# Swapping 32-row halves of a rotary embedding with transfers instead of a matrix product, in an attention layer whose TensorE never rests

## The reference

```python
proj = h @ attn_w_in                       # 2048 -> queries, keys, values, gates
q = rmsnorm(q, q_gain); k = rmsnorm(k, k_gain)          # per head, over 128 features
# of each head: features 0-63 by the token's row, 64-127 by its column;
# in each 64: a = first 32, b = second 32
q = [a * cos - b * sin, b * cos + a * sin]              # the same for k
p = softmax(q @ k.T * scale)                            # then values, a gate, an output product
```

## Time and profile before

| | |
|---|---|
| median of 3 runs | 2449.05 us (2448.95 to 2449.17) |
| profiled execution, first to last instruction | 2448.6 us |
| what lies around the span, against the median | 0.45 us |
| PE busy | 2375.3 us, 97% |
| DVE busy | 1410.8 us, 58% |
| ACT busy | 1171.6 us, 48% |
| POOL busy | 246.5 us, 10% |
| DMA | 402.37 MB, 164 GB/s |

### The profile page before, as it was taken

One profiled execution on the slowest core, in us unless ns is written; L12 is line 12 of the kernel. 1 busy time (PEld: TensorE's weight loads), 2 busy tenths in 40 slices (PEclk: granted clock), 3 DMA queues, 4 the chain that ended last, 5 costly groups with the idle time before them and its releaser, 6 DMA issues.

```text
span 2448.6 us, 43575 instructions
## 1 busy us (share of the span) xinstructions
PE 2375.3 (97%) x17033; PEld 2200.1 (90%) x17033; DVE 1410.8 (58%) x1814; ACT 1171.6 (48%) x1739; POOL 246.5 (10%) x202
## 2 busy tenths in 40 slices
PE   8999999999989999999999989999999989999998
PEld 7897899998879999999988869998889989998876
DVE  5555644458566666666644457885554463555544
ACT  5444544445454444454444444444454453664443
POOL 0000000015001221221200001220002000010210
PEclk9999999999999999999999999999999999999999
DMA  8544466646646556556655545444335555553343
GB/s 288 154 138 134 133 190 186 181 153 199 203 132 195 183 176 193 188 175 192 202 187 188 189 146 159 149 153 121 96 103 173 171 179 164 150 155 104 104 146 138
DMA packets 254407, 402.37 MB, mean 164 GB/s; under 512 B 15136, under 2 KB 111389, under 8 KB 253245
## 3 DMA queue, kind: packets, MB, share of 16 engines
q1 hardware_dynamic: 252452, 393.53, 51.2%
q10 hardware_dynamic: 1832, 7.13, 0.8%
HBM read 396.38 MB, written 4.22 MB: 164 GB/s over the span
## 4 chain that ended last, share of the span: by engine, by line
PE 92%; DVE 4%; ACT 3%; issue 1%; DMA 0%; POOL 0%; ACTq 0%; DVEq 0%; SPq 0%; POOLq 0%
PE bank L1755 63%; PE bank L1852 13%; PE bank L2278 4%; PE bank L1770 2%; DVE wlo L1130 1%; PE bank L2244 1%; PE bank L2069 1%; ACT whi L569 1%; PE bank L2038 1%; PE bank L1795 1%; PE bank L2205 1%; PE bank L2013 0%; PE bank L2007 0%; PE bank L1917 0%; DVE mixtmp L1418 0%
## 5 line engine op out<-in xcount | busy, mean ns | idle before, releaser
L1130 DVE TENSOR_TENSOR wlo<-raw,whi 128x1024 fp32r<-128x1024 f32 x749 | 953.6, 1282 | 832.3 <-ACT whi L569 829.8
L1755 PE MATMUL bank<-ahi,whi 128*128 128x256 f32 (+1 forms) x4224 | 1215.7, 288 | 2.8 <-ACT gg L891 0.9
L1755 PE MATMUL bank<-ahi,wlo 128*128 128x256 f32 (+1 forms) x4224 | 1199.9, 284 | 0.0
L1755 PE MATMUL bank<-alo,whi 128*128 128x256 f32 (+1 forms) x4224 | 1197.4, 283 | 0.0
L569 ACT ACTIVATE whi<-raw 128x1024 fp32r<-128x1024 f32 x749 | 787.8, 1057 | 799.6 <-PE bank L1755 560.4
L1755 PEld LDWEIGHTS bank<-ahi,whi 128*128 128x128 f32 x4224 | 799.5, 189 | 20.0 <-issue 17.1
L1755 PEld LDWEIGHTS bank<-ahi,wlo 128*128 128x128 f32 x4224 | 798.5, 189 | 0.0
L1755 PEld LDWEIGHTS bank<-alo,whi 128*128 128x128 f32 x4224 | 796.2, 188 | 1.4 <-issue 0.2
L1852 PE MATMUL bank<-whi,ghi 128*128 128x512 f32 x352 | 139.0, 395 | 0.0
L1852 PE MATMUL bank<-whi,glo 128*128 128x512 f32 x352 | 139.0, 395 | 0.0
L1852 PE MATMUL bank<-wlo,ghi 128*128 128x512 f32 x352 | 139.0, 395 | 0.0
(11 more groups left out here) (305 smaller groups left out, 2303.8 us busy)
## 6 DMA issues: line engine op xcount, KB each, us to landing
raw<-in_w_up SPq DMA_DIRECT2D x176, 512.0 KB, 4.6
raw<-in_w_in SPq DMA_DIRECT2D x156, 512.0 KB, 3.6
raw<-in_attn_w_in SPq DMA_DIRECT2D x96, 512.0 KB, 3.9
raw<-in_gla_w_in SPq DMA_DIRECT2D x96, 512.0 KB, 3.7
raw<-in_w_down SPq DMA_DIRECT2D x80, 512.0 KB, 4.2
raw<-in_w_out SPq DMA_DIRECT2D x32, 512.0 KB, 4.2
raw<-in_attn_w_out SPq DMA_DIRECT2D x32, 512.0 KB, 3.6
raw<-in_gla_w_out SPq DMA_DIRECT2D x32, 512.0 KB, 3.5
```

The source lines that it names most:

```text
L1130: dve.tensor_tensor(wlo[:, u % RING, :], raw[:, u % RAW, :], whi[:, u % RING, :].bitcast(F32), ALU.subtract).then_inc(wlo_ready, 1)
L1755: mm = pe.matmul(bank[:, base + t, 0:T], w[wp][:, k, col:col + P], rhs(ap, k0 + k), start=begins and k == 0 and (wp, ap) == (0, 0), stop=e ...
```

## The change

The product with `turn` goes. In its place SyncE issues for every head four SBUF-to-SBUF transfers of 32 rows of 272 `fp32` elements (1088 bytes a row, 136 KB in all) from `n2` to a new tile `turned2`, each from the rows that lie 32 away. The signs of the matrix go into the `sin` table. `qk_rotate(p - 1)` moves on VectorE from the even step, ahead of the reciprocal, to the odd step behind it, and reads `turned2` instead of PSUM. The exchanges stand in SyncE's queue behind certain loads (those of odd units, eight units ahead of what VectorE splits), and SyncE waits there for `qk_normed` and `qk_sin`. The loops over trips of `aqk` and `ag` in SyncE's program are unrolled. The wait for the tables goes from TensorE to VectorE. Some semaphores of the start are merged into others without a change of order.

```diff
-    turn = np.zeros((P, P), f32)
...
+    sign = np.where(np.arange(P) % 64 < 32, f32(-1.0), f32(1.0))[:, None]
...
-        "c_cos": np.cos(angle).astype(f32), "c_sin": np.sin(angle).astype(f32), "c_turn": turn,
+        "c_cos": np.cos(angle).astype(f32), "c_sin": np.sin(angle).astype(f32) * sign,
...
 # SyncE
+            def exchange(i, p):
+
+                n = at(p - 3, i, 4)
+                sp.wait_ge(qk_normed, n)
+                if not under(p - 4, i, 4, 2):
+                    sp.wait_ge(qk_sin, at(p - 5, i, 4))
+                for r0 in range(0, P, 32):
+                    r1 = r0 ^ 32
+                    sp.dma_start(turned2[r0:r0 + 32, p % 2, :], n2[r1:r1 + 32, p % 2, :]).then_inc(qk_turned[p % 2], 16)
+
+            def exchanges_beside(ph, i, j):
+
+                if ph not in ("aqk", "av", "ag") or j % 2 == 0:
+                    return
+                t = i + {"aqk": 0, "av": TRIPS["aqk"], "ag": TRIPS["aqk"] + TRIPS["av"]}[ph]
+                trip, p = (t - 2, 3) if j == 1 else (t - 1, (j - 3) // 2)
+                if 1 <= trip <= TRIPS["aqk"]:
+                    exchange(trip, p)
...
                     sp.dma_start(dst, src).then_inc(raw_loaded[u % RAW], 16)
+                    exchanges_beside(ph, i, j)
...
-                if TRIPS[ph] <= 2:
+                if TRIPS[ph] <= 2 or ph in ("aqk", "ag"):
...
 # ScalarE
-                    for t, name in ((cos, "c_cos"), (sin, "c_sin"), (turn, "c_turn")):
+                    for t, name in ((cos, "c_cos"), (sin, "c_sin")):
...
 # VectorE
                 p, odd = divmod(j, 2)
                 if odd:
+                    if not under(p - 5, i, 4, 0):
+                        qk_rotate(p - 1, i)
                     return
-                if not under(p - 5, i, 4, 0):
-                    qk_rotate(p - 1, i)
...
                 if not under(p - 4, i, 4, 2):
-                    dve.wait_ge(qk_turned, at(p - 5, i, 4))
+                    dve.wait_ge(qk_turned[p % 2], at(64 * (p // 2 - 2), i, 128))
...
-                b = 6 + p % 2
-                dve.wait_ge(qk_turned, at(p - 3, i, 4))
-                dve.tensor_tensor(head, bank[:, b:b + 1, 0:T2], sin[:, :].rearrange("p (o t) -> p o t", o=1),
+                dve.wait_ge(qk_turned[p % 2], at(64 * (p // 2 - 1), i, 128))
+                dve.tensor_tensor(head, turned2[:, p % 2:p % 2 + 1, :], sin[:, :].rearrange("p (o t) -> p o t", o=1),
                                   ALU.mult).then_inc(qk_sin, 1)
...
             trip("aqk", 0, after=later_lo(2))
+            dve.wait_ge(rope_in, 32)
...
 # TensorE
-                if not under(p - 5, i, 4, 0):
-                    qk_turn(p - 1, i)
...
-            def qk_turn(p, i):
-                pe.wait_ge(qk_normed, at(p - 3, i, 4))
-                if not under(p - 4, i, 4, 2):
-                    pe.wait_ge(qk_sin, at(p - 5, i, 4))
-                pe.matmul(bank[:, 6 + p % 2, 0:T2], turn[:, :], n2[:, p % 2, :], start=True, stop=True).then_inc(qk_turned, 1)
...
-            pe.wait_ge(rope_in, 48)
...
-                    else:
-                        qk_turn(3, TRIPS["aqk"])
```

More of the change, by code:

```diff
@@ L113, in shape_constants @@
             angle[r0:r0 + 32, :TB] = inv[:, None] * pos.astype(f32)[None]
-    turn = np.zeros((P, P), f32)
-    for d in range(P):
-        if d % 64 < 32:
-            turn[d + 32, d] = -1.0
-        else:
-            turn[d - 32, d] = 1.0
+    sign = np.where(np.arange(P) % 64 < 32, f32(-1.0), f32(1.0))[:, None]
     s, c = np.arange(P)[:, None], np.arange(P)[None]
@@ L230, in two_blocks_kernel @@
         FIRST_GATED = 4
-        qk2, v2, gs2, cos, sin, turn, sq2, rs2, n2, nc2, p2, pT2, nm2, sum2, vt2, z2hi_first, z2lo_first = region(
+        qk2, v2, gs2, cos, sin, turned2, sq2, rs2, n2, nc2, p2, pT2, nm2, sum2, vt2, z2hi_first, z2lo_first = region(
             ("qk2", [P, 24, T2], F32), ("v2", [P, 3, 1024], F32), ("gs2", [P, KD, T2], F32), ("cos", [P, T2], F32),
-            ("sin", [P, T2], F32), ("turn", [P, P], F32), ("sq2", [P, 2, T2], F32), ("rs2", [P, 2, T2], F32),
+            ("sin", [P, T2], F32), ("turned2", [P, 2, T2], F32), ("sq2", [P, 2, T2], F32), ("rs2", [P, 2, T2], F32),
             ("n2", [P, 2, T2], F32), ("nc2", [P, 2, T2], F32), ("p2", [P, 2, 3, T2], F32), ("pT2", [P, 2, 3, T2], F32),
@@ L339, in two_blocks_kernel @@
             sem, "ident_in meta_in first_in small_in lam_in hots_in start_set table_in".split())
-        x_squared, x_root, x_rstd, xn_ready, xn_turned, par_turned, par_ready, meta_turned, meta_taken = map(
-            sem, "x_squared x_root x_rstd xn_ready xn_turned par_turned par_ready meta_turned meta_taken".split())
+        xn_ready, xn_turned, par_turned, par_ready, meta_taken = map(
+            sem, "xn_ready xn_turned par_turned par_ready meta_taken".split())
         lam_prod, lam_sum, lam_exp, lam_ready = map(sem, "lam_prod lam_sum lam_exp lam_ready".split())
@@ L361, in two_blocks_kernel @@
             sem, "tap2 tap1 gelu_done ff_prod ffhi_ready".split())
-        rope_in, qk_sq, qk_sum, qk_root, qk_rstd, qk_normed, qk_turned, qk_cos, qk_sin, qk_done = map(
-            sem, "rope_in qk_sq qk_sum qk_root qk_rstd qk_normed qk_turned qk_cos qk_sin qk_done".split())
+        rope_in, qk_sq, qk_sum, qk_root, qk_rstd, qk_normed, qk_cos, qk_sin, qk_done = map(
+            sem, "rope_in qk_sq qk_sum qk_root qk_rstd qk_normed qk_cos qk_sin qk_done".split())
+        qk_turned = [sem("qk_turned0"), sem("qk_turned1")]
         s2_ready, max2_ready, p2_ready, inv2, p2_scaled, p2_turned, pT2_act, pT2_dve, o2_ready, o2_taken, z2_ready, v2_turned, v2_taken, \
@@ L620, in _ @@
                 act.wait_ge(x_in[tt], 16)
-                act.activation(xn[:, tt, :], xtok[:, tt, :], ACT.Square, accum_out=xsum[:, tt:tt + 1]).then_inc(x_squared, 1)
-                act.wait_ge(x_squared, tt + 1)
-                act.activation(xrstd[:, tt:tt + 1], xsum[:, tt:tt + 1], ACT.Sqrt, bias=eps, scale=1.0 / D).then_inc(x_root, 1)
+                act.activation(xn[:, tt, :], xtok[:, tt, :], ACT.Square, accum_out=xsum[:, tt:tt + 1]).then_inc(xs_squared, 1)
+                act.wait_ge(xs_squared, tt + 1)
+                act.activation(xrstd[:, tt:tt + 1], xsum[:, tt:tt + 1], ACT.Sqrt, bias=eps, scale=1.0 / D).then_inc(xs_root, 1)
             def first_hi(g):
@@ L653, in start_step @@
                 if j == 8:
-                    act.wait_ge(meta_turned, 1)
+                    act.wait_ge(par_turned, PAR_GROUPS + 1)
                     act.activation(xm[:, :, :], bank[:, 4, 0:KD * TM].rearrange("p (k t) -> p k t", k=KD), ACT.Copy)\
@@ L1177, in _ @@
             for tt in range(2):
-                dve.wait_ge(x_root, tt + 1)
-                dve.reciprocal(xrstd[:, tt:tt + 1], xrstd[:, tt:tt + 1]).then_inc(x_rstd, 1)
-                dve.wait_ge(x_rstd, tt + 1)
+                dve.wait_ge(xs_root, tt + 1)
+                dve.reciprocal(xrstd[:, tt:tt + 1], xrstd[:, tt:tt + 1]).then_inc(xs_rstd, 1)
+                dve.wait_ge(xs_rstd, tt + 1)
                 for c0, c1 in (((0, D),), ((0, D // 2), (D // 2, D)))[tt]:
@@ L1248, in x_summed @@
             def x_summed(b, tt):
-                dve.wait_ge(xs_squared, 4 * (b - 1) + 2 * tt + 2)
+                dve.wait_ge(xs_squared, 2 + 4 * (b - 1) + 2 * tt + 2)
                 dve.tensor_reduce(xstat[:, 1, tt:tt + 1], xstat[:, 2 + tt, :], AX.X, ALU.add).then_inc(xs_sum, 1)
@@ L1256, in x_normed @@
                 if c0 == 0:
-                    n = 2 * (b - 1) + tt + 1
+                    n = 2 * b + tt + 1
                     dve.wait_ge(xs_root, n)
@@ L1832, in start_step @@
                         mm = pe.transpose(bank[:, 4, k * TM:(k + 1) * TM], mrow[:, k * P:(k + 1) * P], ident[0:TM, 0:TM])
-                    mm.then_inc(meta_turned, 1)
+                    mm.then_inc(par_turned, 1)
             def rows_of_unit(ph, b, i, j):
@@ L2309, in _ @@
                     low(glo[:, bass.ds(i * 4 + t, 1), :], pr[:, t % 2:t % 2 + 1, :], ghi[:, bass.ds(i * 4 + t, 1), :], act_ready)
-            pool.wait_ge(rope_in, 48)
+            pool.wait_ge(rope_in, 32)
             for n in range(24):
```

## The result

The changed kernel took 2438.03 us (median of 4 runs, 2437.11 to 2438.56) against 2449.11 of the kernel before (4 runs: the three behind the table of before, 2448.95 to 2449.17, and one of 2451.36). The ratio on record is 0.995, with a 95% interval of 0.9938 to 0.9963; the forecast, 2438.1 of 2449.05, was a ratio of 0.9955. By the medians alone the gain is 11.1 us and the time 0.1 us from the forecast. So the direction and the place of the gain were as forecast, and the range was too narrow at its lower end. What can be said of the rest is said further down.

What follows compares the result with a forecast made beforehand. TensorE, busy for 97% of the span, was taken as the bound. 2448.6 - 10.9 for the removed products, with 0 for transfers, VectorE and last head, plus 0.45 around the span gave 2438.1 us; range 2437.2 to 2440.9.

Steps and rivals of the forecast that it cites:

- What the removed product is worth: On TensorE's chain: 24 products with `turn` at 0.455 us each, so 10.9 us go.
- the pair without a turn: First head's pair of units on TensorE, with no turn before it: 6.48 us against 6.93 for every later pair.
- The transfers: SyncE's four issues per head (1.3 us) and the landing (3.6): 4.9 us from `n2`, hidden within 7.75, cost 0.
- the lower bound (3.8): Least time from `n2` to the exchange's landing: issues 1.1 plus landing 2.7 us.
- The load in front: A unit's load ahead of the exchange in SyncE's queue: could add 1.6 us, giving the upper bound of 7.4.
- VectorE's 6.23 us: VectorE's work per head in a new period of 6.48 us: 0.25 to spare, 96% full, not the bound.
- the whole 0.50 of the lock: Time lost between two splits beside GpSimd's product: the same 0.50 us falls on the sine product, sparing the second split.
- The 0.77 us: GpSimd's product of the same size beside a quieter VectorE, against 1.69 us beside the splits.
- The last head: Its exchange has 5.0 us before the first scores, taken at 4.9: costs 0, with 2.4 us as the bound.
- what the prediction had for 5.8: Rival of a late last exchange, before the first scores: 0.8 us added if it takes 5.8; chance 0.08.
- The budget of 7.75 us: Time from the end of `n2` to VectorE's later rotation, within which each head's exchange must land to stay hidden.
- The range: For the median time: 2437.2 (a turn at 0.49 instead of 0.455) to 2440.9 us, holding 0.92.

Runs made afterwards that it cites:

- the changed kernel again: The changed kernel itself, measured a second time with no edit, against the kernel before: median 2439.8 us, ratio 0.9958.
- the rotation early: The changed kernel with `qk_rotate` back on the even step ahead of the reciprocal: 2456.3 us, ratio 1.0022 to the kernel before.
- the exchange two loads later: The changed kernel with each exchange two loads later in SyncE's queue, behind odd units, one head on: 2463.2 us, ratio 1.0052 to the kernel before.
- the exchange one load later: The changed kernel with each exchange one load later in SyncE's queue, behind even units: 2441.3 us, ratio 0.9961 to the kernel before.

## Why the prediction came out as it did

**What the removed product is worth** was right: 24 x 0.455 = 10.9 us, and the stage is 10.9 shorter in the changed kernel and 10.8 longer again when the product is put back. Reading the step from the pair without a turn instead of the instruction's length is what made it exact.

**The transfers** were placed rightly and mis-sized in both terms. An issue takes 0.59 us in the queue, the upper of the two rows taken, not about 0.4; a landing takes 1.9, not 3.6. The two errors cancel in part: 3.8 us instead of 4.9. That this is just the lower bound (3.8) is luck, as the landing alone is below the least row that it was taken from, 2.7. The load in front, for which the bound had 1.6 us, cost nothing in the changed kernel. In the runs with the exchange right behind a later load the landing was 2.8 and 2.9.

**VectorE's 6.23 us** came out as 6.07. The forecast put the whole 0.50 of the lock on the sine product and spared the second split, and that was right; the product pays 0.57. Of the 0.16 less, 0.14 is the step behind the sum: 0.50 from the sum to the reciprocal before (1502.71 to 1503.21), 0.36 from the sum to the split now (1514.76 to 1515.12). The 0.77 us that the prediction took for a GpSimd product alone is of a subtraction (`z2lo_first`), so it is only near to what the product by the cosine would take; no run has that one alone.
The Trainium skill ("SBUF — State Buffer", "SBUF: two separate sides") says that a VectorE instruction with two SBUF inputs and a GpSimd one that reads SBUF shut each other out for a whole instruction. The trace agrees: 1.01 us with GpSimd's product and 0.44 without.

**The last head** had 5.0 us, and its budget was right: with L at 3.8 TensorE didn't wait, with L at 5.9 it waited 0.8, which is what the prediction had for 5.8. The budget of 7.75 us for the others was 0.2 too wide, and nothing hung on it.

**The range.** The lower end, 2437.2, allowed for another price of the turn (0.49) and for nothing else. The differences between executions of one kernel had no term in the range, without a reason, though the prediction itself put the resolution of a measurement at 4.9 us. That is the step that failed, and it is a size. The price of the turn measured 0.455, so its allowance wasn't needed. The executions differ by far more than the 0.9 us allowed: 4.3 us among the 21 runs of the kernel before, 5.1 among the 5 of the changed kernel again (2437.89 to 2442.96), and the first ratio's interval is 3.1 us to each side. Of the 12.2 us that the first ratio gives, 11.1 are the difference of the medians; the kernel before has one run of 2451.36 beside three within 0.22 us of each other, and it pulls the ratio of the means to 0.9952. How the recorded 0.995 weighs the runs isn't shown, so the rest stays open. The second ratio, 0.9958, would have given 2438.8, within the range.

The profiles show one thing that differs between executions. Their 11.8 us is not the difference of the medians either. In every run here whose span is on record 1.7 to 2.0 us lie between the span and the time, mostly 1.8 (2438.56 - 2436.8 in the profiled run of the changed kernel), where the prediction put the profiled span of before beside a median and had 0.45. By that, an estimate, the execution profiled before took 2450.4, more than each of the three in its table. The forecast doesn't suffer, as 2449.05 - 10.9 is 2438.1 as well.

In the two profiled executions the changed kernel reached the first product with ones 1.0 us later than the kernel before (1496.1 against 1495.1); in the experiments, most of which differ from it only behind this point, it is reached between 1494.7 and 1496.6. It got back 1.9 after the stage. They lie in one stretch near the end, with the same instructions in both (window, busy time of PE, PEld, DVE, ACT, POOL, then the granted clock, DMA share and GB/s; first before, then changed):

```profile
2290.00:2340.00 50.00, 46.23 (x335) 40.59 (x334) 24.92 (x34) 21.59 (x31) 10.00 (x5) 0.93 0.24 85
```
```profile
2281.00:2329.00 48.00, 44.19 (x336) 38.67 (x335) 24.87 (x34) 21.59 (x31) 9.97 (x5) 1.00 0.27 89
```

The clock was granted at 0.93 in the one and at 1.00 in the other, and the stretch is 2 us shorter. From the first to the last start of the products of scores by values there (L2244 before, L2249 after) it is 119.3 us before and 117.0 after. In the second profile of the changed kernel the same two starts are 119.4 us apart (2207.2 to 2326.6), with a clock of 0.95 from 2270 to 2345. So the 0.9 us by which the two spans differ beyond the forecast belong to the clock and the start, not to the change. That the clock also sets the differences among the first four runs isn't shown: of their mean clocks, 0.989 belongs to 2438.00 us and 0.992 to 2438.56. Why the clock falls in one execution of the same work and not in another wasn't tried and stays open.

## What to carry to other kernels

When one engine is busy all the time, read the price of an instruction from two places in its chain that differ by that instruction alone; here it held to 0.1 us, twice. When work is moved into transfers, state the time from the producer's end to the consumer's place in its queue, and check it for the last item on its own: the kernel that is 10.9 us faster than before is 5.6 slower than before when the consumer stands one step earlier. For a range of a fraction of a percent, the spread between executions of the same kernel is a term of its own.

## What the runs showed of the hardware

The issue of a 34 KB transfer of 32 rows from SBUF to SBUF held SyncE's queue for 0.59 us, that of a 512 KB load for 0.37 (median of the loads' issues before). The transfer landed 1.9 us after its issue in the changed kernel, and 2.8 to 2.9 in the two kernels that issue it right behind a load.

TensorE's granted clock fell after a long wait: in the run with the rotation early, after 4.2 us of idle time in front of the first scores, the window from 1668 to 1680 us shows

```profile
1668.00:1680.00 12.00, 11.12 (x59) 9.96 (x60) 6.11 (x13) 4.59 (x10) 0.00 (x0) 0.72 0.55 175
1680.00:1700.00 20.00, 20.00 (x137) 16.64 (x136) 11.87 (x24) 9.10 (x24) 0.00 (x0) 1.00 0.37 106
```

that is, the lower of the two levels (1.2 and 2.4 GHz) for a part of it, and the upper again from 1680. The first four scores behind the wait take 2.18 us in the chain instead of 0.92. The scores took 2.9 us longer from first to last (1668.9 to 1836.3) than without the wait (1654.8 to 1819.3 in the changed kernel again). After the 9.2 us wait of the exchange two loads later it was 2.6 longer (1674.8 to 1841.9), after the 0.8 us wait of the exchange one load later 0.1 (1655.8 to 1820.4). A wait for another engine thus cost more than its own length when it was long, though not in proportion.
